# Modulation chunks loaded between the quarters of the memory in the prologue of a two-block transformer kernel

## The chip, the cores and the metric

One core of one Trainium2 chip runs the whole kernel. The metric is the device time of one execution in microseconds; lower is better. TensorE is called PE below, its weight load PEld, VectorE DVE, ScalarE ACT, GpSimd POOL, and SP (SyncE) is the engine that issues every DMA of this kernel.

## The reference, cut to what matters

Two transformer blocks run on 256 tokens of width 1024, in float32. The first normalizes `x`, modulates it with vectors made from a conditioning vector `c`, and projects it. Beside it a memory of 256 tokens is normalized and multiplied by two small matrices, for attention in the second block. The prologue of the kernel holds only this much of the reference:

```python
mod = jax.nn.silu(c) @ w_ada[l] + b_ada[l]            # c (1,1024), w_ada (1024, 6144)
shift1, scale1, gate1, shift2, scale2, gate2 = jnp.split(mod, N_MOD, axis=-1)
h = modulate(rms_norm(x, g_norm1[l]), shift1, scale1)  # needs shift1 and scale1 whole
proj = h @ w_in[l]
...
mem_n = rms_norm_2(mem, mem_norm_g)
...
mkv = mem_n @ w_kv                                     # once with a_mem_kv, once with b_mem_kv
mk = mkv[..., :MEM_DIM]
mv = mkv[..., MEM_DIM:]
```

## The kernel before, in words

Each engine runs a program of its own, written out by hand in the order in which it is to be executed, and the engines meet at semaphores. There is no scheduler: an instruction that waits holds back everything behind it on its engine.

**What the prologue does.** `shift1` and `scale1` are 2 x 1024 numbers, computed in eight modulation chunks, ada 0 to ada 7. Such a chunk is 1 MB of `w_ada` (128 x 2048 f32). For each one ACT multiplies the first two of eight slices by `silu(c)` (`act_ada`; for chunk 0 DVE does it), DVE multiplies and adds the other six and adds two halves (`dve_ada`; the last addition is left out for chunks 6 and 7), and PE sums over partitions by multiplying with a column of ones (`pe_ada`, "sum i" below; for chunks 6 and 7 it has twice the matmuls). After sum 7, DVE makes `shift1`, `scale1` and the gain, and only then can ACT make `h_hi`, the high part of the modulated input, on which every matmul of the first block's projection rests.

**The memory.** `mem` lies in the tile `ub`. ACT makes `mem_g` (memory times gain, in four quarters), PE multiplies it by four memory chunks of 1 MB: c = 0 (mkv_a 0), c = 1 (mkv_a 1), c = 2 (mkv_b 0) and c = 3 (mkv_b 1) in `pe_mkv`. Each is 16 float32 matmuls and is cut into four pieces of four; behind each piece `pe_extra` puts other work: the sums of the modulation chunks by the table `EARLY_SUMS` (key: chunk c, piece), the means of squares (`pe_mean8` for mem and for x, called n1), and `pe_rs_column`, which turns the memory's scale into a column that DVE copies (`dve_rs_column`). Piece p of chunk c is written (c, p).

**PSUM banks.** Memory chunk c is written to bank c % 2, so chunk 2 waits until chunk 0 has been read out (`dve_evac1` to `mkA`), and chunk 3 until chunk 1 has (`act_evac1` to `mvA`). `mkB` and `mvB` are read out of chunks 2 and 3. DVE does this in the program `dve_one` between ada 5 and ada 6 for `mkB`.

**The stream of weights.** SP issues the DMAs in one fixed order, to one queue. The list `order` holds ada 0 to 7 and then, mixed, the chunks of `w_in` and the later modulation chunks; these go through four buffers `raw`, and chunk n is only issued when chunk n-4 has been used up. The memory, its chunks, the constants `con` and the input `X` are put in between by `sp_program` and have no wait of their own. Each transfer of memory or mkv_a 0 is a quarter, 128 rows of 2 KB; a whole chunk has rows of 8 KB.

**After the prologue.** For each chunk of `w_in`, ACT makes a rounded high part (`whi`), DVE the rest (`wlo`), and PE multiplies the three products. DVE also makes `h_lo`, the low part of the input, and goes on with ada 8 and further ones.

Of the kernel before, what the change touches and what calls it, by code (L numbers as in the profile page):

```python
# [166 lines left out]
def build(nc, A, outs):  # L167
    ctx = ExitStack()
    with ctx:
# [352 lines left out]
        NM = 4  # L522
        TOK1 = {("w_in", i) for i in (4, 5, 8, 9)} | {("mkv_a", 1), ("mkv_b", 1)}
# [88 lines left out]
        def act_mem_gain(act):  # L612
            for kt in range(8):
                if kt % 2 == 0:
                    act.wait_ge(*d_mem[kt // 2].at(0))
                act.activation(mem_g[:, kt, :], mem[:, kt, :], ACT.Copy,
                               scale=V("mem_g", kt)).then_inc(*mem_a.tick(kt))
# [28 lines left out]
        def pe_mkv(pe, c):  # L646

            w, b = mkv_w[c], bank[c % 2]
# [26 lines left out]
        def act_evac1(act, c):  # L675
            name, i = ONE[c]
            b = bank[c % 2]
# [31 lines left out]
        def dve_evac1(dve, c):  # L709
            name, i = ONE[c]  # L710
            b = bank[c % 2]
# [42 lines left out]
        def pe_z(pe, p):  # L754
            pe.wait_ge(*evac_a.at(("w_in", p // 2)))
            pe.wait_ge(*evac_a.at(("w_in", 2 + p // 2)))
            if p == 0:
                pe.wait_ge(*misc_v.at("masks"))
            elif p < 3:
                pe.wait_ge(*sb_a.at(("w", p - 1)))  # L760
                if p == 2:
                    pe.wait_ge(*h_lo_made.at(("mix", 1)))
            else:
                pe.wait_ge(*gla_a.at(("ln", 0)))
                pe.wait_ge(*gla_a.at(("ln", 1)))
            x = scores(pe, p, True)
            x.then_inc(*sb_p.tick(("z", p)))
# [222 lines left out]
        def act_one(act):  # L990
# [3 lines left out]
            act_mem_gain(act)  # L994
            act_square8(act, "mem", mem)
            act_ada(act, 1)
            act.wait_ge(*d_x.at(0))
            act_square8(act, "n1", X)
            act_rs(act, "mem", bank[5], rs_m)
            act_ada(act, 2)  # L1000
            act_ada(act, 3)
            act_rs(act, "n1", bank[6])
            act_evac1(act, 1)
            for i in range(4, 8):
                act_ada(act, i)
# [50 lines left out]
        def dve_one(dve):  # L1056
            dve_ada(dve, 0)
            dve_square8(dve, "mem")
            dve_ada(dve, 1)
            dve_square8(dve, "n1")  # L1060
            dve_ada(dve, 2)
            dve_rs_column(dve)
            dve_evac1(dve, 0)
            dve_ada(dve, 3)
# [4 lines left out]
            dve_ada(dve, 4)  # L1069
            dve_ada(dve, 5)  # L1070
            dve_evac1(dve, 2)
# [9 lines left out]
            for kt in range(8):  # L1081
                if kt == 4:
# [6 lines left out]
                                  SUB).then_inc(*h_lo_made.tick(("n1", kt)))  # L1089
            dve_ada(dve, 8)  # L1090
# [62 lines left out]
        EARLY_SUMS = {(0, 3): (0,), (1, 1): (1,), (2, 0): (2,), (2, 2): (3,), (3, 0): (4,), (3, 1): (5,), (3, 2): (6,), (3, 3): (7,)}  # L1153

        def pe_extra(pe, c, piece):
# [17 lines left out]
            if c == 1 and piece == 0:  # L1173
                pe.wait_ge(*d_con0.at(0))
                pe_mean8(pe, "mem", bank[5])
            if c == 1 and piece == 3:
                pe_mean8(pe, "n1", bank[6])
                pe_rs_column(pe)
# [5 lines left out]
        def pe_own(pe, c):  # L1184
            name, i = ONE[c]
            wait_evac1(pe, c - 2)
# [15 lines left out]
        def pe_one(pe):  # L1202
            pe_wake(pe)
            for c in range(NM):
                if c >= 2:
                    wait_evac1(pe, c - 2)
# [2056 lines left out]

        def sp_program(sp):
            sp.dma_start(vec[:, :], A["vecs"]).then_inc(*d_par.tick(0))
            for n in range(len(order)):
                if n == 0:
                    for h in range(4):
                        t2, c2 = slice(2 * h, 2 * h + 2), slice(512 * h, 512 * h + 512)
                        sp.dma_start(mem[:, t2, :], A["memT"][:, t2, :]).then_inc(*d_mem[h].tick(0))  # L3270
                        sp.dma_start(mkv_w[0][:, c2], A["mkv_a"][0][:, c2]).then_inc(*d_mkv0[h].tick(0))
                if n == 2:
                    sp.dma_start(con[:, 0:NFIRST], A["cons"][:, 0:NFIRST]).then_inc(*d_con0.tick(0))
                    sp_mkv(sp, 1)
                    sp.dma_start(X[:, :, :], A["xT"]).then_inc(*d_x.tick(0))
                if n == 4:
# [171 lines left out]
```

## Time and profile before

| | |
|---|---|
| median of 3 runs | 1052.29 us (1052.28 to 1053.61) |
| span of the profiled execution, first to last instruction | 1051.3 us |
| PE / PEld / DVE / ACT busy | 1020.2 / 966.9 / 733.6 / 562.0 us |
| granted TensorE clock, mean | 0.997 |
| matmuls of the first projection begin | 50.4 us |

The profiled execution has no separate time; its span is 1.0 us below the median of the runs, which is what lies around the first and the last instruction. The profile gives start times from the span's start. In a row of the timeline, "xN" merges N records, and the bracket says how long the engine was idle before and what ended that wait. A float32 matmul leaves two records, so "x8" is one piece of four matmuls.

### The profile page before, as it was taken

Reading aid. Unit: us, or ns where it says so; the run is one execution under the profiler, and the core shown is the slowest. Engines: PE = TensorE matmul, PEld = TensorE weight load, DVE = VectorE, ACT = ScalarE, POOL = GpSimd, SP = SyncE. Lnnn points to the kernel's source line nnn. Section 1 sums busy time; section 2 is a strip of 40 time slices with the busy share of each in tenths; the row PEclk is TensorE's granted clock in tenths of the full one; section 3 lists DMA queues with packets and bytes.
Section 4 is the critical chain, followed back from the end, with each engine's and each line's share of the span. In section 5 each row is a group of like instructions: output and inputs, shape, how many; then the busy total and the mean of one; then the engine's idle time right before and its main releaser. Section 6 shows DMA issues by size and latency. Waiting matters only on the chain.

```text
span 1051.3 us, 22984 instructions
## 1 busy us (share of the span) xinstructions
PE 1020.2 (97%) x10004; PEld 966.9 (92%) x10004; DVE 733.6 (70%) x1194; ACT 562.0 (53%) x858; POOL 0.9 (0%) x7
## 2 busy tenths in 40 slices
PE   7999999999999999998999999999999999999996
PEld 6898889999999998986879999999888799999996
DVE  3898677899976667888557566566857665565654
ACT  4456474665565548764236444454667654444541
POOL 0000000000000000000000000000000000000000
PEclk9999999999999999999999999999999999999999
DMA  9978465466645553331005555465224435554541
GB/s 350 398 259 310 172 239 186 176 239 242 229 139 193 203 231 121 126 118 43 4 6 196 199 174 190 140 214 209 101 78 166 170 124 201 191 175 158 194 166 41
DMA packets 31236, 185.82 MB, mean 177 GB/s; under 512 B 3472, under 2 KB 4768, under 8 KB 13984
## 3 DMA queue, kind: packets, MB, share of 16 engines
q1 hardware_dynamic: 31136, 184.36, 49.2%
q8 instruction: 79, 1.29, 0.5%
q14 instruction: 21, 0.17, 0.0%
HBM read 183.29 MB, written 1.05 MB: 175 GB/s over the span
## 4 chain that ended last, share of the span: by engine, by line
PE 87%; DVE 5%; DMA 3%; ACT 3%; issue 1%; SPq 1%; DVEq 0%; ACTq 0%
PE banks L383 47%; PE banks L1390 17%; PE banks L348 3%; PE banks L380 2%; PE banks L660 1%; DMA land<-in_mkv_a 1%; DVE wlo L328 1%; PE banks L1933 1%; PE banks L1574 1%; PE banks L595 1%; PE banks L1923 1%; ACT whi L313 1%; PE banks L663 1%; DMA raw<-in_a_in 1%; DMA raw<-in_w_in 1%
## 5 line engine op out<-in xcount | busy, mean ns | idle before, releaser
L328 DVE TENSOR_TENSOR wlo<-raw,whi 128x2048 fp32r<-128x2048 f32 (+3 forms) x163 | 323.0, 1982 | 169.3 <-ACT whi L313 169.1
L313 ACT ACTIVATE whi<-raw 128x2048 fp32r<-128x2048 f32 (+3 forms) x163 | 270.7, 1663 | 107.4 <-PE banks L1390 73.5
L383 PE MATMUL banks<-h_lo,whi 128*128 128x256 f32 x1376 | 175.1, 279 | 0.0
L383 PE MATMUL banks<-h_hi,wlo 128*128 128x256 f32 x1376 | 173.1, 277 | 0.0
L383 PE MATMUL banks<-h_hi,whi 128*128 128x256 f32 x1360 | 172.1, 279 | 0.1
L383 PEld LDWEIGHTS banks<-h_lo,whi 128*128 128x128 f32 x1376 | 163.9, 187 | 3.2 <-issue 2.6
L383 PEld LDWEIGHTS banks<-h_hi,wlo 128*128 128x128 f32 x1376 | 163.8, 187 | 1.5 <-issue 1.2
L383 PEld LDWEIGHTS banks<-h_hi,whi 128*128 128x128 f32 x1360 | 162.1, 187 | 2.3 <-issue 1.2
L1416 ACT ACTIVATE u<-u 128x256 f32<-128x256 f32 x44 | 18.4, 418 | 124.9 <-DVE u L1470 124.9
L1390 PE MATMUL banks<-m_lo,whi 128*128 128x256 f32 x528 | 73.4, 278 | 0.0
L1390 PE MATMUL banks<-m_hi,wlo 128*128 128x256 f32 x528 | 73.2, 277 | 0.0
L1390 PE MATMUL banks<-m_hi,whi 128*128 128x256 f32 x528 | 73.2, 277 | 0.0
L1390 PEld LDWEIGHTS banks<-m_lo,whi 128*128 128x128 f32 x528 | 66.3, 188 | 0.0
L1390 PEld LDWEIGHTS banks<-m_hi,whi 128*128 128x128 f32 x528 | 66.3, 188 | 0.0
L1390 PEld LDWEIGHTS banks<-m_hi,wlo 128*128 128x128 f32 x528 | 66.3, 188 | 0.0
L1410 ACT ACTIVATE u<-banks,vec 128x256 f32<-128x256 f32 x44 | 22.5, 562 | 46.9 <-PE banks L383 45.4
L407 ACT ACTIVATE ssb<-X 128x256 f32<-128x256 f32 x48 | 19.2, 410 | 39.9 <-DVE X L1501 11.9
L348 PE MATMUL banks<-h_hi,whi 128*128 128x256 f32 x144 | 29.2, 284 | 3.9 <-ACT h_hi L457 1.4
L579 DVE SCALAR_TENSOR_TENSOR adac<-raw,cs,adac 128x256 f32<-128x256 f32 x66 | 27.0, 478 | 3.3 <-ACT adac L551 3.3
L348 PE MATMUL banks<-h_hi,wlo 128*128 128x256 f32 x144 | 28.2, 277 | 0.0
L1487 DVE TENSOR_TENSOR m_lo<-u,m_hi 128x256 fp32r<-128x256 f32 x66 | 27.5, 416 | 0.5
L1426 ACT ACTIVATE m_hi<-u 128x256 fp32r<-128x256 f32 x66 | 26.7, 404 | 2.0 <-DVE u L1484 1.9
(453 smaller groups left out, 1408.8 us busy)
## 6 DMA issues: line engine op xcount, KB each, us to landing
raw<-in_ada SPq DMA_DIRECT2D x24, 1024.0 KB, 6.6
raw<-in_w_up SPq DMA_DIRECT2D x22, 1024.0 KB, 4.8
raw<-in_a_gu SPq DMA_DIRECT2D x22, 1024.0 KB, 4.8
raw<-in_b_gu SPq DMA_DIRECT2D x22, 1024.0 KB, 4.9
raw<-in_w_in SPq DMA_DIRECT2D x12, 1024.0 KB, 6.4
raw<-in_w_down SPq DMA_DIRECT2D x16, 704.0 KB, 4.1
raw<-in_a_in SPq DMA_DIRECT2D x11, 1024.0 KB, 6.3
raw<-in_a_down SPq DMA_DIRECT2D x16, 704.0 KB, 4.1
```

The source lines that it names most:

```text
L313: act.activation(hi_s[k % NSPLIT][:, 0:w], raw[n % NRAW][:, 0:w], ACT.Copy).then_inc(*hi_made.tick(k))
L328: dve.tensor_tensor(lo_s[s][:, 0:w], raw[n % NRAW][:, 0:w], hi_s[s][:, 0:w].bitcast(F), SUB).then_inc(*lo_made.tick(k))
L348: i_ = pe.matmul(b[0:m, j * T:(j + 1) * T], a[:, kt * step + j * m:kt * step + j * m + m], x[:, kt, :], start=o == 0 and j == 0, stop=sp)
L380: i_ = pe.matmul(b[:, j * m:(j + 1) * m], x[:, kt, j * P:j * P + P], a[:, kt * step:kt * step + m], start=st, stop=sp)
L383: i_ = pe.matmul(b[0:m, j * T:(j + 1) * T], a[:, kt * step + j * m:kt * step + j * m + m], x[:, kt, :], start=st, stop=sp)
L407: act.activation(ssb[:, j, :], src, ACT.Square).then_inc(*sq_a.tick((tag, kt)))
L579: x = dve.scalar_tensor_tensor(out=z[kt % 2], in0=wk, scalar=c, in1=z[kt % 2], op0=MUL, op1=ADD)
L1390: x_ = pe.matmul(b[:, 0:T], a[:, kt * P:kt * P + P], x[:, 11 * half + kt, :], start=half == 0 and o == 0, stop=half == 1 and last)
L1410: act.activation(z[:, j, :], b[:, j * T:j * T + T], ACT.Identity, bias=V("b_conv", f), scale=V("w_conv2", f)).then_inc(*up_a.tick((tag, "t ...
L1416: act.activation(z[:, 1, :], z[:, 1, :], ACT.Silu).then_inc(*up_a.tick((tag, "silu", i)))
L1426: act.activation(m_hi[:, i - 2, :], u[(i - 2) % NU][:, 0, :], ACT.Copy).then_inc(*m_hi_a.tick((tag, i - 2)))
L1487: dve.tensor_tensor(m_lo[:, i - 2, :], u[(i - 2) % NU][:, 0, :], m_hi[:, i - 2, :].bitcast(F), SUB).then_inc(*m_lo_v.tick((tag, i - 2)))
```

## The change

It does four things in the prologue and leaves everything else as it was.

1. SP issues ada 0 after the first quarter of memory and weights, ada 1 after the second, and ada 2 ahead of memory chunk 1; the two last quarters and the first constants come between ada 1 and ada 2, X comes after ada 3.
2. ACT and DVE take ada 1 and 2 ahead of the squares of the memory, and the squares of x later; DVE makes `mkB` after the `h_lo` loop.
3. PE takes the sums, the means and the column at other pieces.
4. The four memory chunks have a bank each (0 to 3), so that chunks 2 and 3 wait for no eviction; the two chunks of `w_in` that follow wait for chunks 0 and 1, and the first use of banks 2 and 3 after them (`pe_z`) waits for `mkB` and `mvB`.

```diff
+        def obank(c):
+            return bank[c] if c < NM else bank[c % 2]
...
         def pe_mkv(pe, c):
-            w, b = mkv_w[c], bank[c % 2]
+            w, b = mkv_w[c], obank(c)
...
             if p == 0:
                 pe.wait_ge(*misc_v.at("masks"))
+                wait_evac1(pe, 2)
+                wait_evac1(pe, 3)
...
-            act_mem_gain(act)
+            act_mem_gain(act, 0, 1)
+            act_ada(act, 1)
+            act_mem_gain(act, 2, 3)
+            act_ada(act, 2)
             act_square8(act, "mem", mem)
-            act_ada(act, 1)
+            act_ada(act, 3)
+            act_rs(act, "mem", bank[5], rs_m)
             act.wait_ge(*d_x.at(0))
             act_square8(act, "n1", X)
-            act_rs(act, "mem", bank[5], rs_m)
-            act_ada(act, 2)
-            act_ada(act, 3)
+            act_ada(act, 4)
+            act_evac1(act, 1)
+            act_ada(act, 5)
             act_rs(act, "n1", bank[6])
-            act_evac1(act, 1)
-            for i in range(4, 8):
-                act_ada(act, i)
+            act_ada(act, 6)
+            act_ada(act, 7)
...
             dve_ada(dve, 0)
+            dve_ada(dve, 1)
+            dve_ada(dve, 2)
             dve_square8(dve, "mem")
-            dve_ada(dve, 1)
-            dve_square8(dve, "n1")
-            dve_ada(dve, 2)
+            dve_ada(dve, 3)
             dve_rs_column(dve)
             dve_evac1(dve, 0)
-            dve_ada(dve, 3)
+            dve_square8(dve, "n1")
+            dve_ada(dve, 4)
+            dve_ada(dve, 5)
             dve.wait_ge(*rs_a.at("n1"))
...
-            dve_ada(dve, 4)
-            dve_ada(dve, 5)
-            dve_evac1(dve, 2)
             dve_ada(dve, 6)
             dve_ada(dve, 7)
...
+            dve_evac1(dve, 2)
             dve_ada(dve, 8)
...
-        EARLY_SUMS = {(0, 3): (0,), (1, 1): (1,), (2, 0): (2,), (2, 2): (3,), (3, 0): (4,), (3, 1): (5,), (3, 2): (6,), (3, 3): (7,)}
+        EARLY_SUMS = {(0, 3): (0,), (1, 0): (1,), (1, 2): (2,), (1, 3): (3,), (2, 1): (4,), (3, 0): (5,), (3, 2): (6,), (3, 3): (7,)}
...
-            if c == 1 and piece == 0:
+            if c == 1 and piece == 1:
                 pe.wait_ge(*d_con0.at(0))
                 pe_mean8(pe, "mem", bank[5])
             if c == 1 and piece == 3:
+                pe_rs_column(pe)
+            if c == 2 and piece == 2:
                 pe_mean8(pe, "n1", bank[6])
-                pe_rs_column(pe)
...
-            wait_evac1(pe, c - 2)
+            wait_evac1(pe, c - 4 if c < NM + 2 else c - 2)
...
-                if c >= 2:
-                    wait_evac1(pe, c - 2)
...
+        def sp_memory(sp, h):
+            t2, c2 = slice(2 * h, 2 * h + 2), slice(512 * h, 512 * h + 512)
+            sp.dma_start(mem[:, t2, :], A["memT"][:, t2, :]).then_inc(*d_mem[h].tick(0))
+            sp.dma_start(mkv_w[0][:, c2], A["mkv_a"][0][:, c2]).then_inc(*d_mkv0[h].tick(0))
```

On the DMA queue, from the first instruction of SP: `vec` holds the small vectors, `ub` the memory, `land` the memory chunks, `raw` a modulation chunk. Before:

```order
L3265 DMA vec<-in_vecs 128x386
L3270 DMA ub<-in_memT 128x512
L3271 DMA land<-in_mkv_a 128x512
L3270 DMA ub<-in_memT 128x512
L3271 DMA land<-in_mkv_a 128x512
L3270 DMA ub<-in_memT 128x512
L3271 DMA land<-in_mkv_a 128x512
L3270 DMA ub<-in_memT 128x512
L3271 DMA land<-in_mkv_a 128x512
L287 DMA raw<-in_ada 128x2048 x2
L3273 DMA con<-in_cons 128x132
L3262 DMA land<-in_mkv_a 128x2048
```

And after the change, the same stretch:

```order
L3275 DMA land<-in_mkv_a 128x512
L287 DMA raw<-in_ada 128x2048
L3274 DMA ub<-in_memT 128x512
L3275 DMA land<-in_mkv_a 128x512
L287 DMA raw<-in_ada 128x2048
L3274 DMA ub<-in_memT 128x512
L3275 DMA land<-in_mkv_a 128x512
L3274 DMA ub<-in_memT 128x512
L3275 DMA land<-in_mkv_a 128x512
L3287 DMA con<-in_cons 128x132
L287 DMA raw<-in_ada 128x2048
L3270 DMA land<-in_mkv_a 128x2048
```

Two modulation chunks stood ahead of memory chunk 1 (the last row), and three stand there now; four stood ahead of chunk 2 and four do now.

On PE, memory chunks 1 and 2, from the first matmul of chunk 1 (`const_by_pool` and the like are semaphores). Before:

```order
L660 MATMUL banks<-land,mem_g 128x256 [waits landed_mkv1]
L660 MATMUL banks<-land,mem_g 128x256 x3
L633 MATMUL banks<-squares_mem,con 128x256 [waits square_added_by_dve,landed_con0]
L634 MATMUL banks<-squares_mem,con 128x256
L660 MATMUL banks<-land,mem_g 128x256 x4
L595 MATMUL banks<-one,S 128x1 [waits ada_chunk_scaled]
L595 MATMUL banks<-one,S 128x1
L660 MATMUL banks<-land,mem_g 128x256 x8
L633 MATMUL banks<-squares_n,con 128x256 [waits square_added_by_dve]
L634 MATMUL banks<-squares_n,con 128x256
L639 MATMUL banks<-con,g 128x1 [waits rs_by_act]
```

After the change, from the third piece of chunk 1 on:

```order
L664 MATMUL banks<-land,mem_g 128x256 x4
L643 MATMUL banks<-con,g 128x1 [waits rs_by_act]
L643 MATMUL banks<-con,g 128x1
L599 MATMUL banks<-one,S 128x1 [waits ada_chunk_scaled]
L599 MATMUL banks<-one,S 128x1
L667 MATMUL banks<-mem_g,land 128x256 [waits landed_mkv2]
L667 MATMUL banks<-mem_g,land 128x256 x7
L599 MATMUL banks<-one,S 128x1 [waits ada_chunk_scaled]
L599 MATMUL banks<-one,S 128x1
L667 MATMUL banks<-mem_g,land 128x256 x4
L637 MATMUL banks<-squares_n,con 128x256 [waits square_added_by_dve]
```

The wait for an eviction ahead of chunk 2 is gone; sum 4 (the last L599 pair) now stands in the middle of chunk 2, ahead of two of its pieces and of all of chunk 3.

On DVE, from the column to the start of the gain. Before:

```order
L644 COPY gdec<-banks 128x2
L718 TENSOR_TENSOR mkA<-banks,g 128x512
L579 SCALAR_TENSOR_TENSOR S<-raw,cs,S 128x256 x6
L585 TENSOR_TENSOR S<-S 128x256
L1067 TENSOR_TENSOR ub<-X,rs_t 128x1024 x2
L579 SCALAR_TENSOR_TENSOR S<-raw,cs,S 128x256 x6
L585 TENSOR_TENSOR S<-S 128x256
L579 SCALAR_TENSOR_TENSOR S<-raw,cs,S 128x256 x6
L585 TENSOR_TENSOR S<-S 128x256
L718 TENSOR_TENSOR mkB<-banks,g 128x512
L579 SCALAR_TENSOR_TENSOR S<-raw,cs,S 128x256 x12
L602 SCALAR_TENSOR_TENSOR mod<-banks,vec 128x8
```

After the change:

```order
L648 COPY gdec<-banks 128x2
L722 TENSOR_TENSOR mkA<-banks,g 128x512
L631 TENSOR_TENSOR squares_n<-squares_n 128x1024
L633 TENSOR_TENSOR squares_n<-squares_n 128x512
L583 SCALAR_TENSOR_TENSOR S<-raw,cs,S 128x256 x6
L589 TENSOR_TENSOR S<-S 128x256
L583 SCALAR_TENSOR_TENSOR S<-raw,cs,S 128x256 x6
L589 TENSOR_TENSOR S<-S 128x256
L1078 TENSOR_TENSOR ub<-X,rs_t 128x1024 x2
L583 SCALAR_TENSOR_TENSOR S<-raw,cs,S 128x256 x12
L606 SCALAR_TENSOR_TENSOR mod<-banks,vec 128x8
```

Ada 3 is now ahead of the column, the sums of x's squares are behind it, and `mkB` stands no longer here but ahead of ada 8 (after 16 rows of the `h_lo` loop).

## Rows read from the trace of the kernel before

**Rows 1.** The page: busy time of each engine, its share of the span.

```profile
PE 1020.2 (97%) x10004; PEld 966.9 (92%) x10004; DVE 733.6 (70%) x1194; ACT 562.0 (53%) x858; POOL 0.9 (0%) x7
```

**Rows 2.** The chain that ended last, 0 to 90 us: start, duration, what.

```profile
7.31 12.00 DMA land<-in_mkv_a
19.35 2.63 PE banks L660 x8
21.97 0.85 PE banks L633 x2
...
29.52 0.43 PE banks L633 x2
...
37.82 1.83 PE banks L663 x8
...
45.73 0.79 PE banks L595 x8
```

**Rows 3.** Timeline 0 to 50 us, PE: start, duration, instruction, idle before.

```profile
30.22 0.50 PE L639 MATMUL banks<-con,g 128*128 128x1 f32 x4
31.58 1.99 PE L663 MATMUL banks<-mem_g,land 128*128 128x256 f32 x8 [0.86 <-DVE mkA L718]
33.41 0.50 PE L595 MATMUL banks<-one,S 128*128 128x1 f32 x4
33.78 3.70 PE L663 MATMUL banks<-mem_g,land 128*128 128x256 f32 x16
...
48.18 0.95 PE L595 MATMUL banks<-one,S 128*128 128x1 f32 x8
49.17 0.17 DVE L602 SCALAR_TENSOR_TENSOR mod<-banks,vec 128x8 f32<-128x8 f32 x1 [1.52 <-PE banks L595]
```

**Rows 4.** Timeline 0 to 50 us, DVE and ACT work that waits for a landing.

```profile
10.61 0.91 ACT L616 ACTIVATE mem_g<-ub,vec 128x256 f32<-128x256 f32 x2 [0.39 <-DMA ub<-in_memT]
14.20 0.62 DVE L573 TENSOR_SCALAR S<-raw,cs 128x256 f32<-128x256 f32 x2 [14.20 <-DMA raw<-in_ada]
...
42.44 0.91 ACT L551 ACTIVATE S<-raw,cs 128x256 f32<-128x256 f32 x2 [1.57 <-DMA raw<-in_ada]
```

**Rows 5.** Stretches of the prologue: length, busy, PEclk, DMA share, GB/s.

```profile
2.00:8.00 6.00, 4.96 (x12) 3.44 (x12) 0.00 (x0) 2.41 (x5) 0.00 (x0) 1.00 0.85 236
8.00:12.00 4.00, 4.00 (x14) 3.28 (x14) 0.00 (x0) 3.21 (x7) 0.00 (x0) 1.00 1.06 417
12.00:20.00 8.00, 5.12 (x26) 4.20 (x25) 5.74 (x13) 2.31 (x4) 0.00 (x0) 1.00 1.02 425
20.00:25.00 5.00, 5.00 (x17) 4.10 (x16) 3.45 (x7) 3.15 (x6) 0.00 (x0) 0.66 1.01 424
25.00:39.00 14.00, 13.14 (x69) 11.71 (x68) 11.77 (x26) 4.66 (x12) 0.00 (x0) 1.00 1.01 424
```

**Rows 6.** Timeline 0 to 50 us, DVE: the pieces of its work.

```profile
23.85 1.23 DVE L627 TENSOR_TENSOR squares_n<-squares_n 128x1024 f32<-128x1024 f32 x1 [1.51 <-ACT squares_n L622]
...
25.11 0.69 DVE L629 TENSOR_TENSOR squares_n<-squares_n 128x512 f32<-128x512 f32 x1
25.72 2.46 DVE L579 SCALAR_TENSOR_TENSOR S<-raw,cs,S 128x256 f32<-128x256 f32 x6
28.21 0.42 DVE L585 TENSOR_TENSOR S<-S 128x256 f32<-128x256 f32 x1
...
42.22 0.68 DVE L718 TENSOR_TENSOR mkB<-banks,g 128x512 f32<-128x512 f32 x1
```

**Rows 7.** Timeline 50 to 90 us: DVE's work behind `h_lo`, and who waits for it.

```profile
71.05 0.33 SPq L287 DMA_DIRECT2D raw<-in_w_in  x1
...
77.50 1.92 ACT L313 ACTIVATE whi<-raw 128x2048 fp32r<-128x2048 f32 x1 [2.93 <-DMA raw<-in_w_in]
...
82.92 0.91 PE L792 MATMUL banks<-sW,con 128*128 128x384 f32 x2 [1.34 <-DVE sW L784]
```

**Rows 8.** Stretch 60 to 71 us, where DVE is full: same columns as rows 5.

```profile
60.00:71.00 11.00, 10.41 (x88) 10.00 (x87) 10.90 (x20) 4.91 (x8) 0.00 (x0) 1.00 0.57 209
```

More of the change, by code:

```diff
@@ L610, in build, with act_mem_gain @@
         rs_c = gdec[:, 0:2]
-        def act_mem_gain(act):
-            for kt in range(8):
+        def act_mem_gain(act, *parts):
+            for kt in itertools.chain(*((2 * h, 2 * h + 1) for h in parts)):
                 if kt % 2 == 0:
@@ L676, in act_evac1 @@
             name, i = ONE[c]
-            b = bank[c % 2]
+            b = obank(c)
             if name == "w_in" and i >= 10:
@@ L710, in dve_evac1 @@
             name, i = ONE[c]
-            b = bank[c % 2]
+            b = obank(c)
             if (name, i) not in BY_DVE:
@@ L3267, in sp_program @@
                 if n == 0:
[L3268 to L3271, printed above, removed]
+                    sp_memory(sp, 0)
+                if n == 1:
+                    sp_memory(sp, 1)
                 if n == 2:
+                    sp_memory(sp, 2)
+                    sp_memory(sp, 3)
                     sp.dma_start(con[:, 0:NFIRST], A["cons"][:, 0:NFIRST]).then_inc(*d_con0.tick(0))
+                if n == 3:
                     sp_mkv(sp, 1)
+                if n == 4:
                     sp.dma_start(X[:, :, :], A["xT"]).then_inc(*d_x.tick(0))
-                if n == 4:
                     sp_mkv(sp, 2)
```

## The prediction

> **What bounds the kernel now.** I read the page first: PE is busy 97% of the span [rows 1], so outside the prologue the kernel is paced by PE, and a shift of the point where the projection starts goes to the end of the kernel almost whole, unless a wait behind it takes it up. The change touches only the first 90 us, so the question is which wait ends last there.
>
> Then the chain of waits from 0 to 90 us [rows 2]. It comes from the landing of memory chunk 1 (12.00 us from issue to landing, at 19.35) and from then on it is nearly all PE: pieces, means and sums one behind the other. The timeline of PE [rows 3] confirms it: from 19.35 to 49.13 (48.18 + 0.95, the end of sum 7) PE waits once, 0.9 us for `mkA`, and DVE waits 1.52 us for PE before it can start on the gain. So the last link is PE's chunk 3 with sum 7, not DVE and not the last modulation chunk, which lands at 42.44 [rows 4].
>
> The third view is the table of stretches [rows 5]. The DMA engines are full (share 1.01 to 1.06) from 8 us on to 39 us, at 417 to 425 GB/s. From 2 to 8 us they move 236 GB/s at a share of 0.85. The granted clock of PE is 1.00 in all stretches but 20 to 25 us, where it is 0.66, that is, partly at the lower level of 1.2 GHz. Ahead of that PE was busy for 5.12 of the 8 us from 12 to 20.
>
> **PE's own work from chunk 1 on.** A piece takes 1.83 us at full clock [rows 2], a sum 0.37 us (33.41 to 33.78) [rows 3], a double sum (6 and 7) 0.79, a mean twice 0.43 [rows 2], the column 0.4 (0.50 with its overlap) [rows 3]. Both programs have 12 pieces, sums 1 to 7, two means and one column behind the landing of chunk 1: 12 x 1.83 + 5 x 0.37 + 2 x 0.79 + 4 x 0.43 + 0.4 = 27.5 us. Before: 19.35 + 27.5 + 0.9 (wait for `mkA`) = 47.75, and the end is at 49.13, so the low clock cost 1.4 us. The rows agree: the first piece took 2.63 for 1.83, and one half of a mean 0.85 for 0.43 [rows 2].
>
> **The change part by part.**
>
> *DMA order.* Chunk 1 now stands behind three modulation chunks, where it stood behind two. A chunk of 1.049 MB at 424 GB/s takes 2.47 us [rows 5]. As the engines are full, chunk 1 lands 2.5 us later, at 21.8. Chunk 2 has the same transfers ahead of it as before, and so have chunk 3, ada 6 and ada 7. Against this stands the start: 6 us at 236 instead of 424 GB/s are worth 2.7 us. Rows of 8 KB between the rows of 2 KB may get a part of it back. The bounds are 0 and 2.5; no row shows the mixture that early, and the small quarters already ran at 417 GB/s from 8 to 12 us, together with the first of ada 0, so their size alone isn't the cause. I take 0.6: chunk 1 at 21.2.
>
> *Ada 0 earlier.* It landed at 14.20 [rows 4] and now has about 1.57 MB fewer ahead of it (two-and-a-half quarter pairs and half a chunk that shares the engines), so near 10. DVE starts some 4 us earlier. That buys nothing by itself, because PE is last; ada 6 and 7 can't be handled before they land (42.44 less the 0.6).
>
> *Squares, column, mkA and sum 4.* Here a new wait arises. Behind the column (c = 1, piece 3) PE does sum 3 and two pieces: 0.37 + 3.66 = 4.0 us. Then it waits for ada 4. DVE, from the same column, has the copy (0.2), `mkA` (0.7, by the row of `mkB`), the sums of x's squares (1.95, 23.85 to 25.80) and ada 4 (2.46 + 0.42) [rows 6]: 5.7 us. So PE stands 1.7 us at sum 4, with two pieces of chunk 2, the mean of x and all of chunk 3 queued behind it; the gain waits for these. Bounds: 0 if DVE's copy and squares overlap better than I read, 2.2. The scale of x waits for that mean; DVE goes on with ada 6 about 43 us, done with ada 7 at 48, ahead of PE still.
>
> *Four banks.* The wait of 0.9 us for `mkA` ahead of chunk 2 goes [rows 3]. That it is gone is in the sum below, since the 1.7 us is the whole wait that is left. The added waits at `pe_z` are for `mkB` and `mvB`, both done some ten microseconds earlier: 0.
>
> *mkB behind the `h_lo` loop.* It took 0.68 us where DVE had to hand over to PE anyway [rows 6]. Now it stands where DVE is full: 10.90 of 11 us from 60 to 71 [rows 8]. Behind it are ada 8 and the `wlo` that frees the buffer for the transfer issued at 71.05; ACT waits 2.93 us for its landing and PE 1.34 us at the end of that line [rows 7]. So +0.7 us, with nothing to hide it. The lower bound is 0.
>
> *The clock.* PE now does chunk 0 in four pieces with a landing ahead of each. The last quarter was ready at 10.61 [rows 4] and now comes behind two modulation chunks, near 16 us; PE has 3 pieces and one sum (5.9 us) between 9 and 21.2 us, about half of the time. Before, 5.12 of 8 us of work were followed by the lower level [rows 5]. I take the same loss as before, 1.4 us, as the likeliest. If the slow stretch falls into the waits of chunk 0 it costs nothing; the wait at sum 4 may bring a second one. The Trainium skill, TensorE: Matmul & The Clock Gate, section HAM oscillation, describes such a case: runs of matmuls shorter than the DMA waits between them keep the clock low. By that rule the loss would be paid in chunk 0 too, where it is mostly hidden behind the landings, so the sum stays within the cases here.
>
> **Sum.** 21.2 + 27.5 + 1.4 + 1.7 = 51.8 us for the end of sum 7, against 49.1: +2.7. With `mkB` +3.4. The span of 1051.3 becomes 1054.7; the medians lie 1.0 above it, so 1055.7 us.
>
> **The rivals.**
>
> *The clock stays full in chunks 1 to 3* (the slow stretch is spent in the waits of chunk 0). 1.4 us less: 1054.3, +0.19%, which a measurement can't tell from no change (0.2% or 2.1 us is about its limit). For it: PE at the lower clock would look busier ahead of chunk 1. Against: at least 2 us idle right before it. Chance 0.22.
>
> *A second slow stretch behind the wait at sum 4.* Half a stretch like that of 20 to 25 us again, +1.6: 1057.3. For it: 1.7 us of idle time in the middle of chunk 2. Against: the wait of 0.9 us brought none. Chance 0.2; the likeliest case itself has 0.43.
>
> *The transfers start faster.* All of the 2.5 us is regained in the first 8 us, chunk 1 lands at 19.3, as before. The sum is then 49.9, +0.8, with `mkB` +1.5: 1053.8; with a full clock too 1052.4. For it: the low rate from 2 to 8 us; against it the 417 GB/s right behind, and the first transfers, which stay small. The Trainium skill, DMA: Bandwidth & Descriptors, section Bandwidth, asks for transfers of 1 MiB or more, as smaller ones reach a lower rate; by that rule this rival would be the case, and the trace bears it out only for the first 6 us. Chance 0.08.
>
> *Faster: DVE is the bound, and PE keeps up.* If PE's work did not matter, the path would be the last landing (42.44 less 0.6), ACT 0.91, DVE 2.46 and sum 7 0.95: 46.2 against 49.1, -2.9; with `mkB` -2.2: 1050.1. It decides once PE is through chunk 3 by then, for which chunk 1 would have to land before 18.7 at full clock and with no wait at sum 4 (46.2 - 27.5). 18.7 lies before the old landing, with more bytes ahead. Chance 0.07, with what I overlook.
>
> **How the numbers follow.** Likeliest case and second slow stretch are slower by over 0.2% (0.63). Full clock and fast start lie within 0.2%, 0.30 together (at the edge, the first at +0.19%). Faster has 0.07. The range goes from 1052.3, the fast start with a full clock, to 1057.6, just over the second slow stretch; below lies the faster rival, above a mishap that I don't see. The likeliest case alone reaches from 1054.4 to 1056.6 (wait at sum 4 from 0.6 to 2.2, regained start from 0 to 1.2).
>
> **What would show it.** In the profile of the changed kernel: the first matmul of chunk 1 at 21.2 instead of 19.35, with a DMA as what ended PE's wait; a wait of PE for DVE of about 1.7 us ahead of one sum, between 34 and 38 us, and no wait for `mkA`; sum 7 ending near 51.8; DVE starting its first multiplication near 10 instead of 14.2; the granted clock below 1 for some 3 us near 21 us; the stretch from there to the wait at the old 82.92 longer by 0.7. I am wrong if PE's pieces of chunk 3 are over before 49 us, if chunk 1 lands before 20 us, or if what is lost at 50 us is made up by 90 us.

## The result, and the profile after

The changed kernel is slower: 1056.64 us median (1053.66 to 1061.64, 19 runs) against 1053.61 us (1050.51 to 1058.62, 19 runs) on the same chips, and the ratio of the timed runs is 1.0035, 95% interval 1.0023 to 1.0046, or 3.7 us (2.4 to 4.8). (The two medians alone differ by 3.0 us, which lies within that interval.) The forecast was 1055.7 us against 1052.29, a ratio of 1.0032.

The profiled execution took 1058.9 us, with a span of 1057.1, so it is 2.3 us above the median of its kernel. In every run that has both numbers the time is 1.7 to 1.9 us longer than the span, and not 1.0 as I had read from one span and a median: the profiled execution of before, with its span of 1051.3 us, took about 1053.1 us. Between the two profiled executions lie 5.8 us, more than between the timed runs, so what the traces below show is a dear case of the change. The busy times on the page are nearly those of [rows 1]:

```profile
PE 1020.6 (97%) x10004; PEld 965.7 (91%) x10004; DVE 734.3 (69%) x1194; ACT 561.9 (53%) x858; POOL 0.9 (0%) x7
```

The chain that ended last, 0 to 95 us, answers to [rows 2]:

```profile
8.18 14.25 DMA land<-in_mkv_a
22.47 3.68 PE banks L664 x8
26.49 1.83 PE banks L664 x8
...
36.01 2.47 DVE S L583 x6
38.50 0.43 DVE S L589
38.98 0.61 PE banks L599 x4
39.59 3.42 PE banks L667 x8
```

Memory chunk 1 lands at 22.4 us and its first piece takes 3.68 us, where before it was 2.63; a piece at full clock is 1.83. The chain then goes over DVE's ada 4 into sum 4 (38.98), which it did not do before, and the piece behind that sum is slow again. The timeline of PE shows the waits, and what set them, against [rows 3]:

```profile
22.47 3.68 PE L664 MATMUL banks<-land,mem_g 128*128 128x256 f32 x8 [2.20 <-DMA land<-in_mkv_a]
...
33.74 3.70 PE L667 MATMUL banks<-mem_g,land 128*128 128x256 f32 x16
38.98 0.61 PE L599 MATMUL banks<-one,S 128*128 128x1 f32 x4 [1.54 <-DVE S L589]
39.45 3.56 PE L667 MATMUL banks<-mem_g,land 128*128 128x256 f32 x8
...
53.78 0.95 PE L599 MATMUL banks<-one,S 128*128 128x1 f32 x8
54.77 0.17 DVE L606 SCALAR_TENSOR_TENSOR mod<-banks,vec 128x8 f32<-128x8 f32 x1 [2.69 <-PE banks L599]
```

Sum 7 ends at 54.73 (53.78 + 0.95), before at 49.13. The wait for `mkA` is gone, that for sum 4 has come, 1.54 us. DVE, which began with ada 0 at 10.99 instead of 14.20 [rows 4], waits 2.69 us for PE at the end, 1.2 more than before: its early start was worth nothing. The table of stretches (length, busy, PEclk, DMA share, GB/s), against [rows 5]:

```profile
2.00:8.00 6.00, 3.91 (x10) 2.71 (x9) 0.00 (x0) 2.41 (x5) 0.00 (x0) 1.00 0.84 260
8.00:12.00 4.00, 3.37 (x8) 2.17 (x8) 1.01 (x4) 0.36 (x1) 0.00 (x0) 0.62 1.03 419
...
20.00:25.00 5.00, 2.80 (x9) 2.27 (x9) 3.95 (x8) 2.86 (x5) 0.00 (x0) 0.76 1.00 424
...
39.00:43.00 4.00, 4.00 (x13) 3.25 (x14) 2.73 (x7) 0.00 (x0) 0.00 (x0) 0.58 0.84 319
```

The clock is low in three places where before it was in one: in the gaps of chunk 0, at the start of chunk 1, and right behind the wait at sum 4. The transfers of the first 6 us ran at 260 GB/s for 236.

**The account of the 5.6 us at sum 7 in the two profiled executions.** Chunk 1 starts 3.12 us later (22.47 for 19.35). The waits behind it are 1.54 for 0.86, +0.7. What is left over 27.5 us of PE's work is the cost of the low clock: 54.73 - 22.47 - 27.5 - 1.54 = 3.2 us, before 1.4, +1.8. The sum is 5.6.

These 5.6 us reach the end. The same instruction of ACT, 420 us behind the start of `h_hi`, stands 5.7 us later in the changed kernel, and the span is 5.8 us longer. Before, and then after the change:

```profile
469.83 0.91 ACT L1795 ACTIVATE t<-t,vec 128x256 f32<-128x256 f32 x2 [0.23 <-DVE t L1842]
475.56 0.91 ACT L1803 ACTIVATE t<-t,vec 128x256 f32<-128x256 f32 x2 [0.23 <-DVE t L1850]
```

The time from the start of `h_hi` to this point is the same within 1.5 us in all traces of this document but x7's. Further on it isn't: the next 80 us took 75.9 to 80.6 us from trace to trace, whatever the change. The span of a single trace therefore says little about one change of 1 or 2 us; that is for the timed runs to say.

### The profile page after: what moved, and what is told of

Its sections match the earlier page's. It is cut to its first block, busy times and chain, and to the rows that moved or that the text cites. A ratio compares the mean times of both kernels' runs of the same rounds, so it can differ in the third digit from the quotient of the medians.

```text
span 1057.1 us, 22983 instructions
## 1 busy us (share of the span) xinstructions
PE 1020.6 (97%) x10004; PEld 965.7 (91%) x10004; DVE 734.3 (69%) x1194; ACT 561.9 (53%) x858; POOL 0.9 (0%) x7
## 4 chain that ended last, share of the span: by engine, by line
PE 86%; DVE 6%; DMA 3%; ACT 3%; issue 1%; SPq 1%; DVEq 0%; ACTq 0%
PE banks L383 47%; PE banks L1398 17%; PE banks L348 3%; PE banks L380 2%; PE banks L664 2%; DMA land<-in_mkv_a 1%; DVE wlo L328 1%; PE banks L1941 1%; PE banks L1582 1%; PE banks L1931 1%; PE banks L599 1%; ACT whi L313 1%; DMA raw<-in_a_in 1%; PE banks L1947 1%; PE banks L1908 1%
## 5 line engine op out<-in xcount | busy, mean ns | idle before, releaser
L583 DVE SCALAR_TENSOR_TENSOR adac<-raw,cs,adac 128x256 f32<-128x256 f32 x66 | 27.1, 479 | 3.4 <-ACT adac L555 3.4
L1495 DVE TENSOR_TENSOR m_lo<-u,m_hi 128x256 fp32r<-128x256 f32 x66 | 27.5, 417 | 0.4 <-ACT m_hi L1434 0.2
```

Of the source, the lines that this page charges most:

```text
L583: x = dve.scalar_tensor_tensor(out=z[kt % 2], in0=wk, scalar=c, in1=z[kt % 2], op0=MUL, op1=ADD)
L1495: dve.tensor_tensor(m_lo[:, i - 2, :], u[(i - 2) % NU][:, 0, :], m_hi[:, i - 2, :].bitcast(F), SUB).then_inc(*m_lo_v.tick((tag, i - 2)))
```

## The experiments

Each was timed beside the kernel before on the same chip, with 6 runs of x1 and x10 and 11 or 12 of the others; times are given as a ratio to it, with the 95% interval. Where a trace is quoted it is of one execution, so that the clock of PE differs from trace to trace.

### x1: the queue alone

```diff
                 if n == 0:
-                    for h in range(4):
+                    sp_memory(sp, 0)
+                if n == 1:
+                    sp_memory(sp, 1)
                 if n == 2:
+                    sp_memory(sp, 2)
+                    sp_memory(sp, 3)
                     sp.dma_start(con[:, 0:NFIRST], A["cons"][:, 0:NFIRST]).then_inc(*d_con0.tick(0))
+                if n == 3:
                     sp_mkv(sp, 1)
+                if n == 4:
                     sp.dma_start(X[:, :, :], A["xT"]).then_inc(*d_x.tick(0))
-                if n == 4:
                     sp_mkv(sp, 2)
```

This is the kernel before with the queue of the change.

> The kernel before with the new order of the DMA queue alone; PE, DVE and ACT keep their old orders and the two banks. My theory (memory chunk 1 lands 3 us later and PE's 27.5 us of work start there): first matmul of chunk 1 at 22.4 instead of 19.35, and since the squares of x now wait for X (27.4) ahead of ada 2 on DVE, PE also waits some 2 to 3 us for mkA; sum 7 ends at 52.5 to 56 instead of 49.1, ratio to before 1.003 to 1.006. Rival (the new queue order is harmless, the loss is made by the reordered sums and squares): sum 7 near 49, ratio 1.000.

Ratio 1.0050 (1.0033 to 1.0068). PE's timeline:

```profile
22.05 1.99 PE L660 MATMUL banks<-land,mem_g 128*128 128x256 f32 x8 [2.37 <-DMA land<-in_mkv_a]
...
34.53 3.44 PE L663 MATMUL banks<-mem_g,land 128*128 128x256 f32 x8 [2.03 <-DVE mkA L718]
...
52.58 0.95 PE L595 MATMUL banks<-one,S 128*128 128x1 f32 x8
```

Chunk 1 at 22.05, PE waits 2.03 us for `mkA` and 0.49 for the squares of x, the piece behind the wait is slow, sum 7 ends at 53.5. Against the 49.13 us of before these are +2.7 for the start, +1.2 for the longer wait for `mkA`, +0.5 for the squares and nothing for the clock: 4.4 us. The rival, that the queue is harmless, is out: the queue alone costs about as much as the whole change. Whether the other parts give some of it back isn't resolved, as the intervals overlap. Nor does x1 show the late landing by itself, as two waits for DVE come with it.

### x2: chunk 1 ahead of ada 2

```diff
-            act_ada(act, 2)
             act_square8(act, "mem", mem)
+            act_ada(act, 2)
...
-            dve_ada(dve, 2)
             dve_square8(dve, "mem")
+            dve_ada(dve, 2)
...
-                if n == 3:
                     sp_mkv(sp, 1)
```

> The changed kernel with memory chunk 1 issued ahead of ada 2, and with the squares of the memory ahead of ada 2 on ACT and DVE, so that they are ready for it. My theory: chunk 1 lands 2.5 us earlier (near 20.0), and everything behind it on PE moves with it: sum 7 ends 2.0 to 2.5 us before that of the changed kernel, ratio to before 1.001. Rival (DVE's chain sets the end, not PE's start on chunk 1): sum 7 where it was, ratio 1.0035.

Ratio 1.0039 (1.0024 to 1.0054): not the gain that I expected. PE's timeline:

```profile
15.82 5.38 PE L667 MATMUL banks<-mem_g,land 128*128 128x256 f32 x16 [1.97 <-ACT mem_g L620]
21.40 1.97 PE L664 MATMUL banks<-land,mem_g 128*128 128x256 f32 x8
...
36.20 0.61 PE L599 MATMUL banks<-one,S 128*128 128x1 f32 x4 [1.55 <-DVE S L589]
36.67 3.24 PE L667 MATMUL banks<-mem_g,land 128*128 128x256 f32 x8
```

Chunk 1 no longer waits for its landing, but for PE itself: two pieces of chunk 0 took 5.38 us instead of 3.69, at a low clock, so chunk 1 began at 21.40. A second slow piece follows the wait at sum 4. In this trace sum 7 ends at 51.95, 2.8 us ahead of the changed kernel's; in the timed runs there is no such gain (from end to end the intervals allow one of at most 2.3 us). The trace of x2 lies at the median of its kernel (1057.53 us against 1057.48), that of the changed kernel 2.3 us above, and this may be most of the difference. The rival had this ratio right, but not its reason: DVE isn't the last link here either, it waits 2.70 us for PE at the end. Why the timed runs gained nothing stays open.

### x3: sums 4 and 5 later

```diff
-        EARLY_SUMS = {... (1, 3): (3,), (2, 1): (4,), (3, 0): (5,), (3, 2): (6,), (3, 3): (7,)}
+        EARLY_SUMS = {... (1, 3): (3,), (3, 0): (4,), (3, 1): (5,), (3, 2): (6,), (3, 3): (7,)}
```

> The changed kernel with sum 4 behind the first piece of chunk 3 and sum 5 behind its second. My theory: the wait of 1.5 us for DVE in the middle of chunk 2 goes, and with it the stretch at half clock that follows it in the profiled run (1.7 us); sum 7 ends 1.5 to 3.2 us earlier, ratio to before 1.000 to 1.002. Rival (the wait only moves to the next sum): ratio 1.0035.

Ratio 1.0008 (0.9996 to 1.0020), by the two ratios 2.8 us below the changed kernel. PE's timeline:

```profile
22.25 1.99 PE L664 MATMUL banks<-land,mem_g 128*128 128x256 f32 x8 [0.45 <-DMA land<-in_mkv_a]
...
31.83 5.43 PE L667 MATMUL banks<-mem_g,land 128*128 128x256 f32 x24
...
48.38 0.95 PE L599 MATMUL banks<-one,S 128*128 128x1 f32 x8
```

PE goes through three pieces of chunk 2 in 5.43 us without a stop; sum 7 ends at 49.33, with chunk 1 as late as ever (22.25) and no stretch below full clock behind it up to 50 us; the low clock had come in chunk 0, whose last two pieces took 5.74 us. 49.33 - 22.25 = 27.1 us: that is PE's bare work, estimated at 27.5. The wait did not move to another sum, so the rival is out.

### x4: filler in PE's idle time

`pe_spin(pe, bank, n)` issues n matmuls whose results nobody reads.

```diff
                 for n, _ in enumerate(pe_mkv(pe, c)):
+                    if c == 2 and n == 1:
+                        pe_spin(pe, bank[6], 3)
                     pe_extra(pe, c, n)
+                    if c == 0 and n == 1:
+                        pe_spin(pe, bank[4], 3)
+                    if c == 0 and n == 3:
+                        pe_spin(pe, bank[4], 5)
```

> The changed kernel with idle PE time filled by matmuls whose results nobody reads: 3 behind the second piece of chunk 0, 5 behind sum 0, 3 ahead of sum 4. No result changes. My theory of the clock (idle time ahead of chunk 1 and of sum 4 brings the stretches at the lower clock): no stretch below full clock between 20 and 50 us, sum 7 ends 1.5 to 3.4 us earlier, ratio to before 1.000 to 1.002. Rival (the low stretches don't depend on the idle time, or cost nothing): ratio 1.0035 or more, as the filler only adds work.

Ratio 1.0028 (1.0013 to 1.0042). The table of stretches:

```profile
8.00:12.00 4.00, 3.12 (x8) 2.01 (x8) 1.10 (x4) 0.45 (x2) 0.00 (x0) 0.64 1.04 422
12.00:20.00 8.00, 7.80 (x28) 6.60 (x29) 5.21 (x13) 3.13 (x9) 0.00 (x0) 0.75 1.03 420
20.00:25.00 5.00, 5.00 (x28) 4.46 (x26) 4.01 (x8) 2.88 (x5) 0.00 (x0) 1.00 1.02 429
25.00:39.00 14.00, 13.75 (x74) 12.05 (x73) 10.12 (x24) 6.09 (x12) 0.00 (x0) 1.00 1.01 421
39.00:43.00 4.00, 4.00 (x20) 3.52 (x19) 2.45 (x6) 1.70 (x5) 0.00 (x0) 1.00 0.94 378
```

With PE busy, the clock stays at 1.00 from 20 us on, and the piece behind sum 4 takes 1.97 us where it took 3.56. But the low stretch has come earlier, into chunk 0 (0.64 and 0.75), and made the filler late: chunk 1 began at 23.21, 0.8 us behind its landing. Sum 7 ends at 52.00, 2.7 us earlier than in the changed kernel's trace, while the ratio gained is only 0.0007, not resolved. The clock did what I expected, but that the filler caused it isn't shown: in x8 and x10 the clock stayed full behind the same idle times without any filler. The part of the expectation on the time is open.

### x5: filler in the kernel before

```diff
                 for n, _ in enumerate(pe_mkv(pe, c)):
+                    if c == 0 and n == 3:
+                        pe_spin(pe, bank[4], 3)
                     pe_extra(pe, c, n)
+                    if c == 0 and n == 3:
+                        pe_spin(pe, bank[4], 2)
```

> The kernel before with 3 matmuls whose results nobody reads ahead of sum 0 and 2 behind it, where PE is idle for 1.9 and 1.0 us. No result changes. My theory of the clock: the stretch at half clock from 20.6 to 24.0 us goes, chunk 1 starts where it did (19.35, at most 0.3 later), sum 7 ends 1.1 to 1.6 us earlier, ratio 0.998 to 0.999. Rival (the low stretch costs nothing or comes anyway): ratio 1.000.

Ratio 0.9998 (0.9985 to 1.0012). The filler was too short: PE's timeline still has an idle time of 2.73 us behind it, and the first piece of chunk 1 is slow as ever.

```profile
13.39 1.46 PE L1195 MATMUL banks<-rmask 128*128 128x256 f32 x6
17.58 0.58 PE L595 MATMUL banks<-one,S 128*128 128x1 f32 x4 [2.73 <-DVE S L585]
18.02 1.11 PE L1195 MATMUL banks<-rmask 128*128 128x256 f32 x4
19.14 3.64 PE L660 MATMUL banks<-land,mem_g 128*128 128x256 f32 x8
```

So it tells nothing of what the slow stretch of the kernel before is worth.

### x6 and x7: four banks, without and with the late mkB

x6 is the kernel before with `obank`, no wait ahead of chunks 2 and 3, and the waits of `pe_own` and `pe_z` as in the change. x7 has this edit besides:

```diff
             dve_ada(dve, 5)
-            dve_evac1(dve, 2)
             dve_ada(dve, 6)
...
+            dve_evac1(dve, 2)
             dve_ada(dve, 8)
```

> The kernel before with the four banks alone; queue and all orders as before. My theory: the wait of 0.9 us ahead of chunk 2 goes and nothing replaces it but a short wait for ada 3's sum; sum 7 ends 0.5 to 0.9 us earlier, ratio 0.999 to 0.9995. Rival (DVE's chain of modulation chunks ends at 47.65 and takes the gain up): sum 7 at 49.1 less 0 to 0.3, ratio 1.000.

> As x6 with mkB moved behind the h_lo loop. My theory of the prediction: DVE is full there, so the transfer of the next chunk of w_in is issued 0.6 to 0.7 us later from the start of h_hi (22.0 instead of 21.4) and PE's wait behind it (33.3 us behind the start of h_hi) comes 0.7 later too; ratio 0.0007 above that of x6. Rival (the landing of that transfer is set by the transfers ahead of it on the DMA engines, as the changed kernel's own trace hints with 5.9 us to landing for 6.45): issue 0.6 later, PE's wait at 33.3 as before, ratio as x6.

Ratios 0.9993 (0.9979 to 1.0007) and 0.9998 (0.9984 to 1.0012). The direction is that of my theory for both, the size is below what the runs resolve. The timeline of x6 from the start of `h_hi` to PE's wait:

```profile
48.77 4.05 ACT L1015 ACTIVATE h_hi<-ub,mod 128x256 fp32r<-128x256 f32 x8 [2.23 <-DVE mod L1083]
...
70.19 0.33 SPq L287 DMA_DIRECT2D raw<-in_w_in  x1
...
76.35 1.91 ACT L313 ACTIVATE whi<-raw 128x2048 fp32r<-128x2048 f32 x1 [2.59 <-DMA raw<-in_w_in]
...
81.77 0.91 PE L797 MATMUL banks<-sW,con 128*128 128x384 f32 x2 [0.98 <-DVE sW L789]
```

and that of x7:

```profile
49.02 4.05 ACT L1015 ACTIVATE h_hi<-ub,mod 128x256 fp32r<-128x256 f32 x8 [2.71 <-DVE mod L1082]
...
71.04 0.33 SPq L287 DMA_DIRECT2D raw<-in_w_in  x1
...
78.10 1.92 ACT L313 ACTIVATE whi<-raw 128x2048 fp32r<-128x2048 f32 x1 [3.43 <-DMA raw<-in_w_in]
...
83.51 0.91 PE L797 MATMUL banks<-sW,con 128*128 128x384 f32 x2 [1.94 <-DVE sW L789]
```

With the late `mkB` the transfer is issued 22.02 us behind the start of `h_hi`, without it 21.42. The landing then takes 7.1 us in the one and 6.2 in the other, and PE's wait ends 34.5 and 33.0 us behind the start of `h_hi`.

### x8: sums 4 and 5 late, and mkB where DVE waits

The changed kernel with the table of x3 and this:

```diff
             dve_ada(dve, 7)
+            dve_evac1(dve, 2)
             dve.wait_ge(*ada_p.at(7))
...
-            dve_evac1(dve, 2)
             dve_ada(dve, 8)
```

> The changed kernel with sum 4 and 5 late, as x3, and mkB read out between ada 7 and the wait for its sum, where DVE waits 2.5 us for PE. My theory: sum 7 as in x3 (49.3), the w_in transfer issued 21.4 us behind the start of h_hi as in the kernel before, ratio 0 to 0.0007 below that of x3, which was 1.0008. Rival (mkB there holds back the gain): sum 7 as x3, but h_hi 0.3 us or more later.

Ratio 1.0005 (0.9990 to 1.0020), x3 had 1.0008: in the direction, not resolved. PE's timeline:

```profile
21.50 1.99 PE L664 MATMUL banks<-land,mem_g 128*128 128x256 f32 x8 [2.32 <-DMA land<-in_mkv_a]
```

Chunk 1 starts at 21.50 at full clock, though PE was idle for 2.32 us ahead of it, and sum 7 ends at 48.6: again 27.1 us. The transfer is issued 21.4 us behind `h_hi` again and `h_hi` is not held up.

### x9: memory chunks first

The kernel before with the four banks as in x6, and this:

```diff
-                if n == 2:
+                if n == 1:
                     sp.dma_start(con[:, 0:NFIRST], A["cons"][:, 0:NFIRST]).then_inc(*d_con0.tick(0))
                     sp_mkv(sp, 1)
+                if n == 2:
                     sp.dma_start(X[:, :, :], A["xT"]).then_inc(*d_x.tick(0))
-                if n == 4:
+                if n == 3:
                     sp_mkv(sp, 2)
-                if n == 6:
+                if n == 5:
                     sp_mkv(sp, 3)
...
-        EARLY_SUMS = {(0, 3): (0,), (1, 1): (1,), ...
+        EARLY_SUMS = {(1, 0): (0,), (1, 2): (1,), ...
-            if c == 1 and piece == 0:
+            if c == 1 and piece == 1:
```

> The kernel before with four banks, and with every memory chunk moved towards the front of the queue instead of the modulation chunks: chunk 1 between ada 0 and ada 1, chunk 2 ahead of ada 3, chunk 3 ahead of ada 5. Sum 0 goes behind the first piece of chunk 1, the mean of the memory behind the second, sum 1 behind the third. My theory (PE's start on chunk 1 and its 27.5 us of work set the end): chunk 1 at 16.7 to 16.9, sum 7 ends near 47.2, now held by the last modulation chunks (ada 7 lands at 42.4), 1.9 us before the kernel before, ratio 0.998. Rival (DVE's chain sets the end, so that landings of modulation chunks should come first): sum 7 at 49 or later, ratio 1.000 or more.

Ratio 0.9990 (0.9977 to 1.0002), not resolved from 1, nor from x6, the four banks alone (0.9993). Chunk 1 began at 16.09 at full clock, and sum 7 ended at 48.12, 0.9 us later than I expected. PE's timeline shows why, four waits for DVE:

```profile
33.53 0.61 PE L598 MATMUL banks<-one,S 128*128 128x1 f32 x4 [1.27 <-DVE S L588]
...
38.64 0.61 PE L598 MATMUL banks<-one,S 128*128 128x1 f32 x4 [0.94 <-DVE S L588]
...
41.47 0.61 PE L598 MATMUL banks<-one,S 128*128 128x1 f32 x4 [0.39 <-DVE S L588]
...
44.44 1.05 PE L598 MATMUL banks<-one,S 128*128 128x1 f32 x8 [0.53 <-DVE S L582]
```

Taken this far, the queue makes the modulation chunks late, and PE waits for DVE again and again: what the early start brought is mostly lost. The balance lies between the two orders.

### x10: the changed kernel with the old queue

```diff
                 if n == 0:
-                    sp_memory(sp, 0)
-                if n == 1:
-                    sp_memory(sp, 1)
+                    for h in range(4):
...
-                if n == 3:
                     sp_mkv(sp, 1)
```

> The changed kernel with the DMA queue of the kernel before; all orders of ACT, DVE and PE and the banks as changed. My theory: chunk 1 starts at 19.3 again, but the mean of the memory now stands behind ada 2 (landed 24.3) on ACT and DVE, so PE waits about 5 us at the second piece of chunk 1; sum 7 ends at 54 to 57, ratio 1.004 to 1.006: the orders need the queue. Rival (only the queue order costs): sum 7 at 49 to 50, ratio 1.000 to 1.001.

Ratio 1.0056 (1.0044 to 1.0069), as expected in size, but the wait stands elsewhere. PE's timeline:

```profile
17.89 5.93 PE L667 MATMUL banks<-mem_g,land 128*128 128x256 f32 x16 [7.38 <-ACT mem_g L620]
...
29.97 0.67 PE L637 MATMUL banks<-squares_mem,con 128*128 128x256 f32 x2 [1.80 <-DVE squares_mem L633]
```

ACT now takes ada 1, which lands at 16.4, ahead of the last two quarters of the memory, so PE is idle for 7.38 us in chunk 0, and chunk 1 starts at 24.02 and not at 19.3. At the mean, where I had put 5 us, the wait is 1.80. Sum 7 ends at 54.93. The wait at sum 4 is there as in the changed kernel, but the piece behind it runs at full clock:

```profile
40.86 0.61 PE L599 MATMUL banks<-one,S 128*128 128x1 f32 x4 [1.54 <-DVE S L589]
41.33 1.97 PE L667 MATMUL banks<-mem_g,land 128*128 128x256 f32 x8
```

The rival falls: the changed orders of the engines need the changed queue.

### x11: three mends together

The changed kernel with the edits of x2 (chunk 1 and the memory's squares ahead of ada 2), x3 (sums 4 and 5) and x8 (`mkB`); of each one line:

```diff
-                if n == 3:
                     sp_mkv(sp, 1)
...
+        EARLY_SUMS = {... (1, 3): (3,), (3, 0): (4,), (3, 1): (5,), (3, 2): (6,), (3, 3): (7,)}
...
             dve_ada(dve, 7)
+            dve_evac1(dve, 2)
             dve.wait_ge(*ada_p.at(7))
```

> The changed kernel with memory chunk 1 ahead of ada 2 and the squares of the memory ahead of it (x2), sums 4 and 5 late (x3) and mkB between ada 7 and its sum (x8). My theory: chunk 1 lands at 19.5, no wait at sum 4, so sum 7 ends at 47.5 if PE's clock stays full (DVE and the landing of ada 7 allow 47), and 49.0 if a low stretch falls into chunk 1; ratio 0.997 to 0.999. Rival (the low clock in chunk 0, with its gaps of 2 us between quarters, eats the earlier landing again, as in x2): chunk 1 starts at 21 or later, sum 7 at 48.5 to 49, ratio 1.000.

Ratio 0.9976 (0.9965 to 0.9988): 1050.79 us median (12 runs) against 1053.77 of the kernel before. It beats both kernels, the one before by 2.5 us. PE's timeline:

```profile
16.07 3.69 PE L667 MATMUL banks<-mem_g,land 128*128 128x256 f32 x16 [0.19 <-ACT mem_g L620]
...
19.96 1.97 PE L664 MATMUL banks<-land,mem_g 128*128 128x256 f32 x8
...
46.38 0.95 PE L599 MATMUL banks<-one,S 128*128 128x1 f32 x8
```

Chunk 1 starts at 19.96 and sum 7 ends at 47.33: 27.4 us, with no wait to speak of and no slow stretch behind the start. The low stretch came in chunk 0 here too, where it mostly filled the time between the quarters. Against x3 (0.9996 to 1.0020), which has the late landing, the intervals don't overlap. By the ratios the three edits together bring 6.2 us against the changed kernel, where that of x3 alone brought 2.8, and those of x2 and x8 nothing that is resolved. Part of this may be noise; why they should bring more together than apart isn't shown.

## Why the prediction was right

**PE's start on memory chunk 1, and 27.5 us of work behind it, set the end of the prologue.** Shown for this path: where nothing stopped PE, it took 27.1 us (x3, x8) and 27.4 us (x11), and DVE waited for PE at the end in each of them. That the end of the prologue then sets the time of the kernel is seen over all kernels. In us against the kernel before, the end of sum 7 in the one trace, and the ratio of the timed runs times 1053.6:

| | after | x1 | x2 | x3 | x4 | x5 | x6 | x7 | x8 | x9 | x10 | x11 |
|---|---|---|---|---|---|---|---|---|---|---|---|---|
| sum 7 | +5.6 | +4.4 | +2.8 | +0.2 | +2.9 | -0.3 | -0.9 | -0.6 | -0.6 | -1.0 | +5.8 | -1.8 |
| timed | +3.7 | +5.3 | +4.1 | +0.8 | +3.0 | -0.2 | -0.7 | -0.2 | +0.5 | -1.1 | +5.9 | -2.5 |

They agree within 1.9 us, and the changed kernel's own trace is the furthest off.

**Chunk 1 lands one transfer later, less 0.6 us that the start gives back.** Direction right, the second term wrong. Kernels with the new queue began chunk 1 at 22.47, 22.05, 22.25 and 21.50 (changed, x1, x3, x8), those with the old one ahead of it at 19.35, 18.80 and 19.30 (before, x6, x7): +2.9 us on the mean, where I had put +1.9 and one transfer is 2.5. The starts differ by 0.6 and 1.0 us within the two groups, so 2.9 isn't clear of 2.5, but none of the 0.6 us is seen to come back. The rate from 2 to 8 us did rise, from 236 to 260 GB/s (over all traces 225 to 265 with the old order of the first transfers, 260 to 293 with the new), but nothing of it is seen at chunk 1. What this later start costs by itself is in part argued: x11 against x3 speaks for it, x2 against the changed kernel doesn't. The rival of a faster start, and with it the rule of the Trainium skill (DMA: Bandwidth & Descriptors, section Bandwidth) as I had applied it, is not borne out. What happens to those first transfers in detail was not tried.

**A wait of 1.7 us at sum 4.** Shown: 1.54 us, one row of the trace, with the ada 4 of DVE as what ended it. Its removal (x3) brought 2.8 us, more than the wait itself; that the rest is the clock behind the wait fits the traces and isn't shown.

**The clock.** I took one slow stretch of 1.4 us as before and gave a second one behind sum 4 a chance of 0.2. In the profiled execution of the changed kernel the second came, and PE's low clock cost 3.2 us in all. It came behind a wait for DVE in x1 and x2 too, but not behind the same wait at sum 4 in x10; in x3 there is no such wait, and in x4 there is filler in its place. The stretch of before at the start of chunk 1 I had taken over. Of the traces with the new queue (those of x2 and x11 with chunk 1 ahead of ada 2 included) only that of the changed kernel has it; in x1 and x8 chunk 1 started at full clock, and in x2, x3, x4 and x11 the low clock came in chunk 0. So the clock differs from trace to trace, and how often each case comes in runs that are not profiled isn't shown. For the changed kernel there is a hint: its time behind the prologue is an ordinary one (1001.9 us from `h_hi` to the end, where the thirteen traces have 999.5 to 1005.1), so the 2.3 us above its median probably lie in the prologue. Sum 7 of a median execution would then end near 52.4 us (an estimate, 54.73 less 2.3), which would fit one slow stretch and not two; I had forecast 51.8.

**mkB behind the h_lo loop, +0.7 us.** The first half is shown: the `w_in` transfer is issued 22.0 us behind `h_hi` in the changed kernel and x7, 21.4 in those of before, x6 and x8. In all thirteen traces it is 22.0 us with the late `mkB` and 21.4 us without. The second half isn't shown for the time: the landing takes 5.2 to 7.1 us from trace to trace, and in the changed kernel's own trace PE came to its wait 33.4 us behind `h_hi`, as before (33.3 [rows 7]). In x7 against x6 it was 1.5 us later, while the ratios differ by 0.0005 and those of x3 and x8 by 0.0003, neither resolved. On the mean of the traces PE comes to that point 33.6 us behind `h_hi` with the late `mkB` and 32.9 without, which has the size that I expected, with a spread as large as itself.

**The sum, and luck in it.** The sum of 3.4 us had one term too small (the landing, by 1.0) and one of 0.7 that no timed run resolves (`mkB`). The two errors nearly cancel, and that 3.4 lies so near 3.7 is in part luck; the interval of 2.4 to 4.8 would also bear other sums. Against the one trace the end of sum 7 was forecast 2.9 us too early, 1.3 by the start of chunk 1 and 1.8 by the clock, less 0.2 by the wait. Some figures of the prediction were off without bearing on the outcome. The medians lie 1.8 and not 1.0 us above a span. The bounds given for the likeliest case add up to 1054.0 to 1056.8 us, not 1054.4 to 1056.6. And the 1.57 MB that ada 0 no longer has ahead of it are three pairs of quarters.

**Four banks.** Costs nothing at `pe_z`, and takes away the 0.9 us wait; by itself 0.9993, not resolved.

**DVE's head start is worth nothing because PE is last.** Right for the changed kernel: DVE waits 2.69 us at the end. But in x11, where PE has been freed, DVE is done with ada 7 at 45.9, just ahead of sum 7, and PE reaches sum 7 at 46.4. As I read it, the head start is what makes 47.3 possible; x9 lacks it and waits for DVE. That the two have to go together is what I had not seen.

## What to carry to other kernels

When transfers share one full queue, moving one forward moves those that it overtakes back by about its length (here chunk 1 by 2.9 us for a transfer of 2.5 us). Ask which engine sets the end and what it waits for, and place that transfer first, then the orders of the engines that feed it. A consumer's small sum put in the middle of long work of the last engine should stand where its producer has surely finished: moving sum 4 by three pieces and sum 5 by one gave back some three quarters of what the whole change cost (2.8 of 3.7 us). With both of these and `mkB` moved, the change made the kernel 0.24% faster instead of 0.35% slower.

## What the runs showed of the hardware

A wait of PE can be dearer than its length, but isn't always. From the landing of chunk 1 on, PE waited nine times for 1.5 to 2.4 us in the traces of the changed kernel, x1, x2, x8, x9 and x10. Behind four of these waits the granted clock was at the lower level of 1.2 GHz, and the next piece took 3.2 to 3.7 us, where it takes 1.97 to 1.99 at full clock: 2.20 and 1.54 us in the changed kernel, 2.03 in x1, 1.55 in x2. Behind the other five it was at full clock, 2.4 GHz: 2.37 us in x1, 2.32 in x8, 2.41 in x9, 1.80 and 1.54 in x10. The length of the wait doesn't tell the two apart. The Trainium skill, TensorE: Matmul & The Clock Gate, section HAM oscillation, tells of a low clock behind waits for DMAs; here it came behind waits for another engine too. A low stretch can also come early, in gaps that would be idle anyway, and then costs little (x3, x11); in x2 it came early and still held chunk 1 back.
